# A two-layer hybrid decoder trunk: three-pass products for the latents and the embedding, with roots applied later, two-pass sums, host-laid columns and a unit in halves

## What is computed

```python
for i in range(2):
    h = rms_norm(x, attn_norm[i])            # x * rsqrt(mean(x*x) + eps) * gain
    proj = h @ w_in[i]
    # A: stick-breaking attention
    log_keep = where(mask, log_sigmoid(-z), 0)
    tail = cumsum(shifted(log_keep), reverse=True)
    w = where(mask, exp(log_sigmoid(z) + tail), 0)
    # B: latents of 192 and 128 columns, each normed, then their up products
    c_q, c_kv = rms_norm(mla[:, :192], g), rms_norm(mla[:, 192:320], g)
    q_m, kv_m = c_q @ mla_w_uq[i], c_kv @ mla_w_ukv[i]
    ...
    x = x + concat(groups) @ w_o[i]
    x = x + gated_mlp(rms_norm(x, ffn_norm[i]))
    x = x + sigmoid(x @ ple_gate[i]) * (p[i] @ ple_proj[i])
```

## Time and profile before

| | |
|---|---|
| median of 3 runs | 709.52 us (709.22 to 710.29) |
| profiled execution, its own time | 710.84 us |
| its span, first to last instruction | 709.1 us |
| TensorE busy, share of the span | 98% |
| VectorE, ScalarE, GpSimd busy | 47%, 55%, 55% |
| mean granted TensorE clock | 0.997 |

### The profile page before, as it was taken

The page is one execution under the profiler, slowest core; times in us unless marked ns, Lnnn a source line. Parts: engine busy times, 40 slices in busy tenths (PEclk is TensorE's granted clock), DMA queues, the critical chain, the costliest instruction groups (busy, mean ns, idle before and its releaser), DMA issues.

```text
span 709.1 us, 11731 instructions
## 1 busy us (share of the span) xinstructions
PE 691.7 (98%) x4628; PEld 622.6 (88%) x4628; DVE 331.2 (47%) x548; ACT 390.4 (55%) x578; POOL 388.7 (55%) x213
## 2 busy tenths in 40 slices
PE   4999999999999999999999999999999999999997
PEld 3889998789999999998858999886999999999985
DVE  3746676545433333335165576666343333333333
ACT  4658675466544445555346596546655445545542
POOL 4431200157888888888720222011698888887781
PEclk9999999999999999999999999999999999999999
DMA  9962212465565555554366511326455555555511
GB/s 292 350 226 90 90 60 83 157 229 189 187 196 194 189 178 177 178 184 145 108 208 213 190 60 62 118 82 215 144 183 194 193 179 177 178 183 195 184 31 59
DMA packets 78884, 116.11 MB, mean 164 GB/s; under 512 B 2343, under 2 KB 66727, under 8 KB 78591
## 3 DMA queue, kind: packets, MB, share of 16 engines
q1 hardware_dynamic: 77598, 112.46, 48.0%
q10 hardware_dynamic: 1248, 3.15, 1.1%
HBM read 114.55 MB, written 1.05 MB: 163 GB/s over the span
## 4 chain that ended last, share of the span: by engine, by line
PE 90%; DVE 3%; POOL 3%; ACT 2%; DMA 1%; issue 1%; SPq 0%; DVEq 0%; ACTq 0%
PE ps L859 23%; PE ps L861 23%; PE ps L860 23%; PE ps L874 3%; PE ps L1210 2%; POOL wl L418 2%; PE ps L943 2%; PE ps L980 2%; PE ps L908 1%; PE ps L963 1%; DMA ng<-norm_gains 1%; PE ps L934 1%; PE ps L973 1%; DVE pb L1708 1%; ACT wh L539 1%; DVE wl L1441 1%
## 5 line engine op out<-in xcount | busy, mean ns | idle before, releaser
L418 POOL TENSOR_TENSOR wl<-raw,wh 128x2048 fp32r<-128x2048 f32 (+1 forms) x72 | 324.5, 4539 | 88.0 <-ACT wh L539 88.0
L539 ACT ACTIVATE wh<-raw 128x2048 fp32r<-128x2048 f32 (+1 forms) x102 | 187.6, 1846 | 113.9 <-PE ps L861 107.9
L859 PE MATMUL ps<-hT_h,wh 128*128 128x256 f32 x752 | 213.2, 284 | 0.1
L860 PE MATMUL ps<-hT_l,wh 128*128 128x256 f32 x752 | 212.8, 283 | 0.0
L861 PE MATMUL ps<-hT_h,wl 128*128 128x256 f32 x752 | 212.8, 283 | 0.0
L859 PEld LDWEIGHTS ps<-hT_h,wh 128*128 128x128 f32 x752 | 144.3, 192 | 2.0 <-issue 0.9
L860 PEld LDWEIGHTS ps<-hT_l,wh 128*128 128x128 f32 x752 | 144.3, 192 | 0.6
L861 PEld LDWEIGHTS ps<-hT_h,wl 128*128 128x128 f32 x752 | 144.3, 192 | 0.0
L405 POOL TENSOR_SCALAR st<-st 128x2 f32<-128x2 f32 (+3 forms) x26 | 9.0, 345 | 160.0 <-ACT lat L586 74.6
L859 PE MATMUL ps<-wh,hT_h 128*128 128x256 f32 (+1 forms) x284 | 93.1, 328 | 0.0
L1708 DVE SCALAR_TENSOR_TENSOR pb<-ps,conv,pb 128x255 f32<-128x255 f32 (+1 forms) x96 | 39.7, 475 | 109.6 <-ACT pb L794 109.3
(11 more groups left out here) (235 smaller groups left out, 895.7 us busy)
## 6 DMA issues: line engine op xcount, KB each, us to landing
raw<-w_up SPq DMA_DIRECT2D x44, 1024.0 KB, 5.1
raw<-w_down SPq DMA_DIRECT2D x22, 1024.0 KB, 4.9
raw<-w_in SPq DMA_DIRECT2D x16, 1024.0 KB, 9.0
raw<-w_o SPq DMA_DIRECT2D x6, 1024.0 KB, 4.9
raw<-ple_gate SPq DMA_DIRECT2D x6, 1024.0 KB, 4.8
raw<-w_in SPq DMA_DIRECT2D x4, 704.0 KB, 6.2
ng<-norm_gains ACTq DMA_DIRECT2D x2, 1024.0 KB, 6.5
raw<-w_o SPq DMA_DIRECT2D x4, 512.0 KB, 3.5
```

Of the source, the lines that this page charges most:

```text
L418: pool.tensor_tensor(wl[:, slot, 0:n], raw[:, slot, 0:n], wh[:, u % RING, 0:n].bitcast(F32), ALU.subtract).then_inc(ffn_l_made, 1)
L539: act.activation(wh[:, u % RING, 0:n], raw[:, slot, 0:n], ACT.Copy).then_inc(h_made, 1)
L859: pe.matmul(dst, a_h, b_h, start=start, stop=False, skip_group_check=True)
L860: pe.matmul(dst, a_h, b_l, start=False, stop=False, skip_group_check=True)
```

## The change

- **Late roots.** x itself is transposed. turned() on vector multiplies the transposed x by the norm's gain (a column per block of 128, gcol, laid out on the host) while it is read out of PSUM into hT; the root is applied to the products: rooted() on scalar (ACT.Identity with the root as the scale) for all that has tokens on the partitions, sb_rooted() on vector for the transposed queries and keys, by a row of roots (rrow) that a product of -1s by a diagonal of -root makes. The gain's broadcast loads go. The squares and x_root stay, later.
- **In layer 1** tensor takes x's quarters between parts of the latents' product, and two of turned() stand in vector's b = 2 step of layer 0.
- **Third unit in halves.** SB_Q's high and low parts are made for 4 blocks at a time. SB_K's product is cut in two, and the latents' transposes stand between. The small loads of layer 0 stand behind unit 2.
- **Up products in three passes**: high parts on scalar, low parts on vector, for the latents (cT_h, cT_l) and the weights (uq, ukv).
- **Two-pass sums.** -1 and 0 are exact in reduced f32, so only softplus is split: high part on scalar, low part on vector, two passes.
- **Embedding's product in three passes**: parts of p and of the unit, on scalar and vector.
- **Host-laid columns.** The conv taps and p come in the layout in which they are used; their transposes go.

```diff
-            sp.dma_start(ng[:, 0:D], norm_gains[0, 0:D].partition_broadcast(P)
-                         ).then_inc(F["gain_landed"], 16)
...
-                    if layer == 0 and u == M_MLA_B:
+                    if layer == 0 and u == M_SB_Q:
...
+                if layer:
+                    pool.wait_ge(F["tables"], layer + 1)
+                    pool.memset(uq[QR - P:P, 1, :], 0.0).then_inc(F["uq_zero"], 1)
+                    pool.wait_ge(F["uq_zero"], layer)
+                for t in range(TT):
+                    x_root(0, t)
...
+                    if halves:
+                        c = n // 2
+                        act.activation(wh[:, u % RING, 0:c], raw[:, slot, 0:c], ACT.Copy
+                                       ).then_inc(F["sbq_high"], 1)
+                    act.activation(wh[:, u % RING, c:n], raw[:, slot, c:n], ACT.Copy
...
+                def rooted(dst, src, t, name, n, done):
+
+                    if name == "unit":
+                        unit_done(act, layer, n)
+                    else:
+                        act.wait_ge(F[name], base[name] + n)
+                    act.activation(dst, src, ACT.Identity, scale=stat(ST_X + 6 + t)
+                                   ).then_inc(F[done], 1)
...
-                x_high(0, AT_START, (0, 1))
+                x_high(0, AT_START)
+                high(M_SB_Q, halves=True)
+                if layer == 0:
+                    act.wait_ge(consts_made, 12)
+                    for o, t in ((neg_tri_r, neg_tri), (neg_ones_r, neg_ones)):
+                        act.activation(o[:], t[:], ACT.Copy).then_inc(signs_made, 1)
...
+                act.dma_start(pT[:], p_cols[layer]).then_inc(F["p_landed"], 16)
+                act.dma_start(conv[:], conv_cols[layer]).then_inc(F["conv_landed"], 16)
+                act.wait_ge(F["roots"], base["roots"] + 2)
+                for t in range(TT):
+                    rooted(pr[:, 0, t, 0:MLA_COLS], ps[:, t, 0:MLA_COLS], t, "unit", M_MLA_B,
                            "pr_ready")
...
+                act.wait_ge(F["uq_landed"], base["uq_landed"] + 16)
+                act.wait_ge(F["uq2_landed"], base["uq2_landed"] + 16)
+                act.wait_ge(F["ukv_landed"], base["ukv_landed"] + 16)
                 if layer == 0:
-                    act.wait_ge(consts_made, 16)
-                for rows, heads in EVEN_ODD:
-                    copied(qk_sb[rows, heads, :],
-                           ps[rows, 2, :].rearrange("p (k n) -> p k n", k=2),
-                           "unit", M_SB_Q, "sbT_ready", scale=HD ** -0.5)
-                copied(pT[:], ps[:, 6, :].rearrange("p (k n) -> p k n", k=2), "p_T", 1, "pT_ready")
+                    act.wait_ge(consts_made, 13)
+                else:
+                    act.wait_ge(F["uq_zero"], layer)
+                for o, w in ((uq_h, uq), (ukv_h, ukv)):
+                    act.activation(o[:], w[:], ACT.Copy).then_inc(F["up_high"], 1)
...
+                for b in range(3):
+                    act.wait_ge(F["sb_soft"], base["sb_soft"] + b + 1)
+                    act.activation(sp_h[b], sb_sp[:, b * 512:(b + 1) * 512], ACT.Copy
+                                   ).then_inc(F["sp_high"], 1)
+                mT_out(0)
                 high(8)
...
+                act.wait_ge(F["p_landed"], base["p_landed"] + 16)
+                act.activation(pT_h[:], pT[:], ACT.Copy).then_inc(F["proj_high"], 1)
+                act.wait_ge(raw_landed[U_PROJ % DEEP],
+                            (layer * (UNITS // DEEP) + U_PROJ // DEEP + 1) * 16)
+                act.activation(proj_h[:], raw[:, U_PROJ % DEEP, :], ACT.Copy
+                               ).then_inc(F["proj_high"], 1)
...
+                if layer == 0:
+                    x_T(x, AT_START, None)
+                    project_tile(M_MLA_A, 0, (0, 1), 0, quarters=0)
+                    project_tile(M_MLA_A, 1, (0, 1), 0, quarters=0)
+                    project_tile(M_MLA_B, 0, (0, 1), 0, quarters=1)
+                else:
+                    x_T(x, AT_START, None, quarters=(0, 1))
+                    project_tile(M_MLA_A, 0, (0, 1), 0, quarters=0)
+                    x_T(x, AT_START, None, quarters=(2,))
+                    project_tile(M_MLA_B, 0, (0, 1), 0, quarters=1, part=(0, 1))
+                    x_T(x, AT_START, None, quarters=(3,))
+                    project_tile(M_MLA_B, 0, (0, 1), 0, part=(2, 3))
+                    project_tile(M_MLA_A, 1, (0, 1), 0, quarters=0)
                 project_tile(M_MLA_B, 1, (0, 1), 0, quarters=1)
...
+                pe.wait_ge(F["sbq_low"], base["sbq_low"] + 1)
+                project_T(M_SB_Q, 2, blocks=range(0, KT // 2), halves=True)
+                project_T(M_SB_Q, 2, blocks=range(KT // 2, KT))
+                pe.wait_ge(F["diag_made"], base["diag_made"] + 1)
+                pe.matmul(ps[:, 7, 256:512], neg_ones[:], tmp[:, 768:1024], start=True,
+                          stop=True, skip_group_check=True).then_inc(F["row_root"], 1)
+                project_T(M_SB_K, 3, columns=(0,))
...
+                    for k in range(2):
+                        split_product(o, cT_h[:, k, tok], cT_l[:, k, tok], uq_h[:, k, :],
+                                      uq_l[:, k, :], k == 0, k == 1)
+                    split_product(ps[:, 5 + 2 * t, :], cT_h[:, 2, tok], cT_l[:, 2, tok],
+                                  ukv_h[:], ukv_l[:], True, True).then_inc(F["mla_up"], 1)
...
+                pe.wait_ge(F["sp_low"], base["sp_low"] + 3)
                 for b in range(2):
                     for j in range(2):
                         i = 2 * b + j
                         h = PAIRED[i]
                         o = ps[:, 4 + b, j * 256:(j + 1) * 256]
-                        pe.matmul(o, neg_tri[:], sb_sp[:, i * 256:(i + 1) * 256], start=False,
-                                  stop=False, skip_group_check=True)
-                        mm = pe.matmul(o[:, P:256], neg_ones[:],
-                                       sb_sp[:, 1024 + h * P:1024 + (h + 1) * P], start=False,
+                        pe.matmul(o, neg_tri_r[:], sp_h[b][:, j * 256:(j + 1) * 256],
+                                  start=False, stop=False, skip_group_check=True)
+                        pe.matmul(o, neg_tri_r[:], pt_r[:, i * 256:(i + 1) * 256],
+                                  start=False, stop=False, skip_group_check=True)
+                        pe.matmul(o[:, P:256], neg_ones_r[:], sp_h[2][:, h * P:(h + 1) * P],
+                                  start=False, stop=False, skip_group_check=True)
+                        mm = pe.matmul(o[:, P:256], neg_ones_r[:],
+                                       pt_r[:, 1024 + h * P:1024 + (h + 1) * P], start=False,
                                        stop=True, skip_group_check=True)
                     mm.then_inc(F["sb_minus"], 1)
-                pe.matmul(ps[:, 6, :], neg_tri[:], sb_sp[:, 1024:1536], start=False, stop=True,
+                pe.matmul(ps[:, 6, :], neg_tri_r[:], sp_h[2], start=False, stop=False,
...
+                        mm = split_product(ps[:, PROJ_BANKS[n], :], pT_h[:, k, tok],
+                                           pT_l[:, k, tok], proj_h[:, c], wl[:, slot, c],
+                                           k == 0, k == 1)
...
+                pe.wait_ge(F["proj_low"], base["proj_low"] + 2)
                 project_p(0)
                 group_T(3)
...
+            def turned(layer, k):
+
+                base = before(layer)
+                t, half = divmod(k, 2)
+                dve.wait_ge(F["xT_ready"], base["xT_ready"] + k + 1)
+                c = slice(4 * half, 4 * half + 4)
+                tt(hT[:, c, t * P:(t + 1) * P],
+                   ps[:, AT_START[k], :].rearrange("p (k n) -> p k n", k=4),
+                   gcol[:, layer, c].unsqueeze(2).broadcast_to([P, 4, P]), ALU.mult
+                   ).then_inc(F["hT_ready"], 1)
...
+                    for k in range(4):
+                        turned(layer, k)
+                else:
+                    for k in range(2, 4):
+                        turned(layer, k)
+                x_low(0, AT_START)
                 if layer == 0:
                     rope_angles()
-                for half in range(2):
-                    dve.wait_ge(F["xT_ready"], base["xT_ready"] + 2 + half + 1)
-                    dve.tensor_copy(hT[:, 4 * half:4 * half + 4, P:SEQ],
-                                    ps[:, AT_START[2 + half], :].rearrange("p (k n) -> p k n", k=4)
-                                    ).then_inc(F["hT_dve"], 1)
-                x_low(0, AT_START, (2, 3))
-                low(2)
+                low(M_SB_Q, halves=True)
+                dve.wait_ge(F["roots"], base["roots"] + 2)
+                for t in range(TT):
+                    last = ts(tmp[:, 768 + t * P:768 + (t + 1) * P], ident[:],
+                              stat(ST_X + 6 + t), -1.0, ALU.mult, ALU.mult)
+                last.then_inc(F["diag_made"], 1)
...
```

(60 more changed lines are left out.)

215 lines of the change are left out of this document (102 added, 113 removed).

## The result

The changed kernel takes 699.13 us (four runs, 697.44 to 699.40) beside 709.37 us for the kernel before (708.64 to 710.29): a ratio of 0.9857, interval 0.9845 to 0.9870. The forecast was 694.4 with a range of 690.7 to 699.6. The time lies in the range, but the gain is 10.2 us and not 15.1.

A forecast was written before the change was run, and what follows sets the result against it. TensorE, busy 691.7 of 709.1 us, was taken to bound the kernel. Gains of 8.35 us in layer 0 and 6.75 in layer 1, together 15.1, off the median 709.52 gave 694.4 us, range 690.7 to 699.6.

The forecast's parts named there:

- The start (4.4): Start of layer 0: TensorE begins the latents' product at 9.0 and ends at 19.7, gain 4.4 us (2.4 to 5.4).
- rival (a): Clock: layer 0's half speed counts anew from 9.0 and layer 1's stays; 698.3 us, chance 0.12.
- the boundary's 3.3: Layer boundary: layer 1's latents' product starts 1.6 us earlier at full speed, gain 3.3 us (1.4 if the clock drops).
- From the latents to SB_K (2.5): Latents' product to SB_K's end: 12.6 us in all, gain 1.5 us in layer 0 and 1.0 in layer 1.
- It just fits: SB_K's low part comes 6.1 us after the latents' product ends; TensorE wants it at 6.2.
- Up products (0.85): Six up products in three passes take 3.45 us instead of 4.30, gain 0.85 us a layer.
- Sums (1.0): Two-pass stick-breaking sums: gain 1.0 us a layer, set by the side engines, between 0 and 1.6.
- short wait for ScalarE ahead of the stick-breaking product: Sign in layer 0: TensorE waits shortly for ScalarE ahead of that product, at 72.3.
- Embedding (0.6): Embedding's product in three passes, 1.37 us each behind a 0.6 wait: gain 0.6 us a layer (0 to 1.4).
- (b): Side engines take back what the passes save, 4.9 us over both layers; 699.3 us, chance 0.08.
- (c): Slower: each new TensorE wait drops the clock, 3.1 us each; ten make 725 us, chance 0.03.
- (d): No new wait and cheap ends at the start, sums and embedding; 691.0 us, chance 0.06.

The follow-up runs named there:

- The run with nine products: Changed kernel plus nine short products of ones that nothing reads, six ahead of the first transposes and three behind them; median 697.70 us.
- last run: Changed kernel plus nine products of ones, embedding's low parts earlier, small loads behind SB_K, SB_K's high and low parts in halves; 694.39 us, ratio 0.9785 to the kernel before.

## Why the forecast was too low

**The start (4.4): the mechanism held, the half speed was mis-sized.** The first transpose came at 4.31, the product at 9.03, as forecast. The text chose 3.5 records at half speed, counted from the first transpose, and an end at 19.7. No profiled execution did that: either none is (SB_Q at 18.33, gain 5.7) or the product takes 2.3 us longer (SB_Q at 20.49, gain 3.5), and six of eight executions belong to the longer group. The upper end that it named, 21.8, and the lower one, 18.7, held both. So the first half of rival (a) came true in most executions: TensorE is not at full speed when the product begins, though transposes ran before it. The run with nine products shows the cause, 1.4 us in the median.

**The frame.** The sum was made against the profiled execution of before (710.84) and taken off the median (709.52) as it stood. That execution had a half-speed stretch in layer 1, some 1.8 us, which by their clock most others don't have; the boundary's 3.3 took it as a gain of the change. For the median the boundary is worth nearer 1.5 to 2, and the 1.5 us between this execution and the median of before is the second largest step that failed; the clock 0.997 in the table before the prediction was the sign to ask for it. Together with the start it makes the 3.2 us between executions. The boundary's own ends, 372.1 and 368.9, give 3.2 and not 3.3.

**From the latents to SB_K (2.5): failed, the largest step.** The lead grew by 0.29 and 0.22 (0.49 and 0.42 from the second pass of SB_Q). "It just fits" was said of SB_K's low part with a margin of 0.1, and two terms ate it. The first was put at nothing: "The copies out of PSUM with a root cost what the copies cost." They don't (ScalarE, layer 0 before, then layer 1 after):

```profile
24.14 0.82 ACT L559 ACTIVATE pr<-ps 128x352 f32<-128x352 f32 x2 [2.58 <-PE ps L874]
24.84 0.89 ACT L625 ACTIVATE rot<-pr 128x352 f32<-128x352 f32 x2
```

```profile
361.26 1.00 ACT L596 ACTIVATE pr<-ps,st 128x352 f32<-128x352 f32 x2 [2.73 <-PE ps L914]
362.15 0.88 ACT L662 ACTIVATE rot<-pr 128x352 f32<-128x352 f32 x2
```

The squares start 0.89 instead of 0.70 us after the first copy, and VectorE's low part ends 6.29 us after the product's last record instead of 6.10. That alone is over the margin, and in layer 1 no load is late beside it. The second is in layer 0 alone: SB_K landed at 21.2 and not by 20, its high part began 0.62 late and its low part ended at 25.6. Against a kernel without the wait (last run) the stage is 0.9 longer in layer 0 and 0.4 in layer 1; there SB_Q and SB_K take 12.85 us from first to last record, or 12.65 without the 0.2 by which SB_Q's first record stands early, as the 12.6 of the sum had it. The other quarter of a us is that before took 13.5 in layer 1 by its first records (372.08 to 385.57), not 13.6, and roundings.

**Up products (0.85): right**, 0.78 measured: 32.10 to 35.62, 3.5 us for 3.45. Four passes against three would have made it 1.07, and the four products of the embedding 1.7 in a layer; the rows had 0.85 and 1.4, and were nearer to the 0.78 and 1.4 that the runs show.

**Sums (1.0): 0.76 by undoing, mechanism partly other.** TensorE's part lasts 2.38 us, as the sum had it (2.3), with a wait ahead that moves it by 0.33. Undoing shows 1.10 for the passes and this 0.33 against them. A pass with 128 columns was taken as 0.11; two of them stand in a row, and the rows give another split of the same sum:

```profile
64.41 0.28 PE L1130 MATMUL ps<-pt_r,neg_tri_r 128*128 128x256 f32 x1
64.52 0.22 PE L1132 MATMUL ps<-gT_l,neg_ones_r 128*128 128x128 f32 x1
64.58 0.27 PE L1134 MATMUL ps<-pt_r,neg_ones_r 128*128 128x128 f32 x1
64.69 0.34 PE L1128 MATMUL ps<-gT_h,neg_tri_r 128*128 128x256 f32 x1
64.86 0.28 PE L1130 MATMUL ps<-pt_r,neg_tri_r 128*128 128x256 f32 x1
```

The first starts its follower after 0.06 and the second after 0.11, but the 256-column pass behind them takes 0.17 instead of 0.12, so the pair costs 0.22 all the same. The short wait for ScalarE ahead of the stick-breaking product, a sign that the prediction named, did not come: the product began at 72.34, and the list of waits has none there.

**Embedding (0.6): 0.20.** The wait was foreseen as 0.6 and was 0.57 in the record; that it moves the passes by 0.84 was not. The passes themselves save the 1.4 of the sum, up to the transposes of x; but the head of the FFN kept 0.39, where the sum had 0.2. 1.4 - 0.84 - 0.39 leaves the 0.2. Place and cover of the wait were named, only the two prices were off.

**Rivals.** (b), side engines take back what the passes save, 699.3, is nearest in time. Undoing shows that the three product changes are worth 0.78, 0.76 and 0.20 a layer at the next stage, 3.5 in all instead of 4.9, so its mechanism is there for sums and embedding, where waits for low parts cost 0.33 and 0.84 a layer; but it is 1.4 of the 4.9 that are missing, and that the time is near 699.3 is chance. (c) fell for this change: waits of 0.2 to 1.1 us left the clock alone. But its mechanism exists: at 4.6 us (low parts on GpSimd) the clock fell to 0.50. Its price, 3.1, was high against the 1.8 that the half speed at the boundary cost before. (d) fell with the waits.

**The sum again.** In the profiled executions: start +1.3, boundary +0.3, SB_K -2.0, up -0.15, sums and embedding -1.2 against the forecast, together -1.7; between executions -3.2; 15.1 - 4.9 = 10.2. Counted from the second pass of SB_Q it is start +1.1, boundary +0.1, SB_K -1.6. The time lies 0.5 below the upper end of the range, which rival (b) had set. That this end was wide enough is luck in part: no rival within the range had priced SB_K's low part or the frame.

## What to carry to other kernels

Take a gain off the median only after asking whether the profiled execution is like the median: its own time against it, and its mean clock, say so. A margin of 0.1 us on an engine that others feed is a wait; a copy that gains an operand is not the same copy, so read its price before it is put at nothing. Price a wait by the distance between passes: here waits booked with 0.57, 0.17 and 0.16 cost 0.84, 0.33 and 0.4. And when a short wait of the bound engine stands behind another engine's long instruction, look for that engine's idle gaps, and halve the instruction to fit them.

## What the runs showed of the hardware that was not expected

The issue of a load can be held up on its queue, and that need not delay the data. Behind the two halves of x and three units the sync queue needed 4.28 us for an issue that took 0.86 before the change, and SB_K's issue stood behind it (the chain that ended last: start us, us, what):

```profile
3.35 4.28 SPq L295
...
9.38 11.85 DMA raw<-w_in
21.25 1.92 ACT wh L565
23.27 2.30 DVE wl L1513
25.61 0.39 PE ps L900
```

But the DMA engines were busy all through from 8 to 24 us (a share of 1.06 and more in every stretch of 2 us), and with the small loads behind SB_K the same hold-up (4.36 us) fell on SB_K's own issue and its weights landed at 17.1, 3.0 us behind those of SB_Q, 1 MB at some 350 GB/s. So the bytes ahead of it, more than the hold-up, seem to set the landing; no run takes the hold-up alone away.

TensorE can begin its first long product at half speed in one execution and at full speed in the next, of the same program, 2.3 us apart, with the granted clock's column at 1.00 in both; with products of ones in idle time none of 22 executions was of the longer kind. A GpSimd instruction of 4.59 us held up a VectorE instruction of 0.16 us for 3.85 us. And in reduced f32 the first of two passes with 128 columns starts its follower after 0.06 us, but the pass behind the pair comes 0.05 late.
